# One transfer, one high part, one low part and one release for each 1 MB weight piece, in place of two halves

## What is computed

```
for l in range(2):                                    # first kind
    h = rms_norm(x, norm1_g[l])
    q, k, v, gu, gv = split(h @ w_in[l])              # 2048 x 3584
    mixed = concat(window attention of q, k, v; spatial gating of gu, gv)
    x = x + mixed @ w_o[l]                            # 2048 x 2048
    x = x + (silu(g) * u) @ w_down[l]                 # 5632 x 2048
        # g, u = split(depthwise_conv(rms_norm(x) @ w_up[l]))   2048 x 11264
# second kind, once: modulation rows from silu(c) @ w_ada (2048 x 12288),
# h @ w_in_2, a Hyena branch (FFT convolution) and an SSD scan,
# @ w_out_2, then relu(n @ w_mlp1)^2 @ w_mlp2 with 8192 hidden features
```

## Time and profile before

| | |
|---|---|
| three runs, median (lowest to highest) | 3502.82 us (3501.29 to 3503.66) |
| profiled execution, its own time | 3501.27 us |
| span of the profile | 3499.5 us |
| PE busy | 3407.4 us, 97% of the span, 15842 matmuls |
| DVE busy | 2373.2 us, 68% |
| ACT busy | 1618.5 us, 46% |
| read from HBM | 689.15 MB, 199 GB/s over the span |

### The profile page before, as it was taken

How to read it: one execution, slowest core, us unless ns; L and a number is a source line. 1 busy time by engine, 2 the same in 40 slices (tenths; PEclk the granted TensorE clock), 3 DMA queues, 4 the chain that set the end, 5 groups by cost and what they waited for, 6 DMA issues and landing times.

```text
span 3499.5 us, 43122 instructions
## 1 busy us (share of the span) xinstructions
PE 3407.4 (97%) x15842; PEld 2805.7 (80%) x15842; DVE 2373.2 (68%) x2974; ACT 1618.5 (46%) x2146; POOL 32.5 (1%) x28
## 2 busy tenths in 40 slices
PE   8999999999999999999999999999999999999998
PEld 6888888887778888888887887777866788888886
DVE  5667888888666666777777676676676655556565
ACT  5555555455334555555555444234432544444443
POOL 0000000000000000000000000000000000000000
PEclk9999999999999999999999999999999999999999
DMA  7557777776677557777777773346603566666664
GB/s 256 147 178 222 222 224 228 228 223 217 223 227 222 150 177 220 223 228 232 233 229 239 256 247 113 101 150 198 216 19 127 168 215 207 210 207 214 200 221 156
DMA packets 369459, 697.56 MB, mean 199 GB/s; under 512 B 25487, under 2 KB 37792, under 8 KB 368672
## 3 DMA queue, kind: packets, MB, share of 16 engines
q1 hardware_dynamic: 368628, 695.25, 62.9%
q10 hardware_dynamic: 684, 0.28, 0.0%
HBM read 689.15 MB, written 6.29 MB: 199 GB/s over the span
## 4 chain that ended last, share of the span: by engine, by line
PE 64%; issue 22%; DVE 6%; DMA 3%; ACT 2%; DVEq 2%; ACTq 0%; POOL 0%; SPq 0%; POOLq 0%
PE acc L2185 16%; PE acc L2187 16%; PE acc L2186 16%; PE acc L2473 3%; PE acc L2475 3%; PE acc L2474 3%; DMA w_raw<-in_w_down 2%; DVE w_lo L1320 2%; PE turn L2395 1%; DVE ada_sum L1424 1%; PE turn L2206 1%; PE turn L2222 1%; ACT w_hi L825 1%; DVEq L1416 1%; PE acc L2685 1%
## 5 line engine op out<-in xcount | busy, mean ns | idle before, releaser
L1320 DVE TENSOR_TENSOR w_lo<-w_raw,w_hi 128x1024 fp32r<-128x1024 f32 x708 | 838.4, 1221 | 372.9 <-ACT w_hi L825 336.2
L825 ACT ACTIVATE w_hi<-w_raw 128x1024 fp32r<-128x1024 f32 x708 | 739.0, 1062 | 718.2 <-DMA w_raw<-in_w_up 317.4
L2185 PE MATMUL acc<-w_hi,in_h 128*128 128x512 f32 x1408 | 552.7, 393 | 0.0
L2187 PE MATMUL acc<-w_hi,in_l 128*128 128x512 f32 x1408 | 548.6, 390 | 0.0
L2186 PE MATMUL acc<-w_lo,in_h 128*128 128x512 f32 x1408 | 548.1, 389 | 0.0
L2124 DVE TENSOR_TENSOR w_lo<-w_raw,w_hi 128x1024 fp32r<-128x1024 f32 x252 | 303.4, 1223 | 196.1 <-ACT w_hi L1284 186.3
L1284 ACT ACTIVATE w_hi<-w_raw 128x1024 fp32r<-128x1024 f32 x252 | 265.0, 1060 | 332.2 <-DMA w_raw<-in_w_mlp 331.6
L2473 PE MATMUL acc<-w_hi,in_h 128*128 128x512 f32 x992 | 394.7, 398 | 8.4 <-DVE in_l L2100 4.3
L2474 PE MATMUL acc<-w_lo,in_h 128*128 128x512 f32 x992 | 388.3, 391 | 0.8 <-issue 0.8
L2475 PE MATMUL acc<-w_hi,in_l 128*128 128x512 f32 x992 | 388.5, 392 | 0.0
L1424 DVE SCALAR_TENSOR_TENSOR ada_sum<-w_raw,silu_c,ada_sum 128x512 f32<-128x512 f32 x450 | 327.6, 750 | 31.0 <-issue 7.0
(11 more groups left out here) (365 smaller groups left out, 4714.6 us busy)
## 6 DMA issues: line engine op xcount, KB each, us to landing
w_raw<-in_w_up SPq DMA_DIRECT2D x352, 512.0 KB, 3.8
w_raw<-in_w_mlp SPq DMA_DIRECT2D x256, 512.0 KB, 3.7
w_raw<-in_w_in SPq DMA_DIRECT2D x200, 512.0 KB, 3.7
w_raw<-in_w_ada SPq DMA_DIRECT2D x192, 512.0 KB, 4.2
w_raw<-in_w_down SPq DMA_DIRECT2D x176, 512.0 KB, 5.0
w_raw<-in_w_o SPq DMA_DIRECT2D x64, 512.0 KB, 3.7
w_raw<-in_w_out SPq DMA_DIRECT2D x32, 512.0 KB, 3.9
K<-k_store SPq DMA_DIRECT2D x16, 256.0 KB, 6.5
```

Of the source, the lines that this page charges most:

```text
L825: nc.scalar.activation(hi[s][:, ks], raw[s][:, ks], ACT.Copy).then_inc(w_hi[s][h], 1)
L1320: nc.vector.tensor_tensor(lo[s][:, ks], raw[s][:, ks], hi[s][:, ks].bitcast(F32), ALU.subtract).then_inc(w_lo[s][h], 1)
L2185: nc.tensor.matmul(acc[p][i][:], high(kt)[:, tok], hi[s][:, k], start=(kt == first), stop=False)
L2187: last = nc.tensor.matmul(acc[p][i][:], low(kt)[:, tok], hi[s][:, k], start=False, stop=(kt == final))
```

## The change

Each slot has one semaphore of each kind. A piece is loaded by one transfer of 1 MB, its high part is one ACT instruction of 128x2048 elements, its low part one DVE instruction of 128x2048, PE waits once ahead of the 24 matmuls and releases the slot once behind them. DVE's ada work still stands in two halves at the same two visits, but both wait for, and the slot is released with, the whole piece. The matmuls and their order are the same. (The small dt piece keeps two transfers.)

```diff
-    w_loaded = [[sem(f"w_loaded{s}_{h}") for h in range(2)] for s in range(NS)]
+    w_loaded = [sem(f"w_loaded{s}") for s in range(NS)]
...
         def piece(src, s, r, n=4):
-            for h in range(2):
-                ks = slice(2 * h, min(2 * h + 2, n))
-                sp.wait_ge(w_free[s][h], r)
-                sp.dma_start(raw[s][:, ks], src[:, ks]).then_inc(w_loaded[s][h], 16)
+            sp.wait_ge(w_free[s], r)
+            sp.dma_start(raw[s][:], src).then_inc(w_loaded[s], 16)
...
         def split_hi(s, r, n=4):
-            for h in range(2):
-                ks = slice(2 * h, min(2 * h + 2, n))
-                act_.wait_ge(w_loaded[s][h], r * 16)
-                nc.scalar.activation(hi[s][:, ks], raw[s][:, ks], ACT.Copy).then_inc(w_hi[s][h], 1)
+            act_.wait_ge(w_loaded[s], r * 16)
+            nc.scalar.activation(hi[s][:], raw[s][:], ACT.Copy).then_inc(w_hi[s], 1)
...
         def split_lo(s, r, n=4):
-            for h in range(2):
-                ks = slice(2 * h, min(2 * h + 2, n))
-                dve.wait_ge(w_hi[s][h], r)
-                nc.vector.tensor_tensor(lo[s][:, ks], raw[s][:, ks], hi[s][:, ks].bitcast(F32), ALU.subtract).then_inc(w_lo[s][h], 1)
+            dve.wait_ge(w_hi[s], r)
+            nc.vector.tensor_tensor(lo[s][:], raw[s][:], hi[s][:].bitcast(F32), ALU.subtract).then_inc(w_lo[s], 1)
...
             for k in range(2 * half, 2 * half + 2):
                 dve.drain()
-                if k == 2 * half:
-                    dve.wait_ge(w_loaded[s][half], r * 16)
+                if k == 0:
+                    dve.wait_ge(w_loaded[s], r * 16)
...
-            a.then_inc(w_hi[s][half], 1)
-            dve.drain().then_inc(w_lo[s][half], 1)
-            dve.sem_inc(w_free[s][half], 1)
+            if half == 1:
+                a.then_inc(w_hi[s], 1)
+                dve.drain().then_inc(w_lo[s], 1)
+                dve.sem_inc(w_free[s], 1)
...
-                if k % 2 == 0:
-                    pe.wait_ge(w_lo[s][k // 2], r)
+                if k == 0:
+                    pe.wait_ge(w_lo[s], r)
...
-                if k % 2 == 1:
-                    last.then_inc(w_free[s][k // 2], 1)
+            last.then_inc(w_free[s], 1)
```

More of the change, by code:

```diff
@@ L284, in program @@
     t_free = [sem(f"t_free{b}") for b in range(2)]
+    dt_loaded = sem("dt_loaded")
     x_in, ctx_loaded = [sem(f"x_in{c}") for c in range(4)], sem("ctx_loaded")
@@ L730, in _ @@
                 s, r = ring(FIRST[j])
-                for h in range(2):
-                    sp.wait_ge(w_free[s][h], r)
-                    sp.dma_start(dt_view(raw[s], h), w_in_b[h * D // 2:(h + 1) * D // 2, col:col + 32].rearrange("(k p) n -> p k n", p=P)).then_inc(w_loaded[s][h], 16)
+                sp.wait_ge(w_free[s], r)
+                for h, done in enumerate((w_loaded[s], dt_loaded)):
+                    sp.dma_start(dt_view(raw[s], h), w_in_b[h * D // 2:(h + 1) * D // 2, col:col + 32].rearrange("(k p) n -> p k n", p=P)).then_inc(done, 16)
                 filter_moves(FIRST[j])
@@ L1116, in split_hi2 @@
             s, r = ring(n, q)
-            for h in range(2):
-                act_.wait_ge(w_loaded[s][h], r * 16)
-                v = (lambda w: dt_view(w, h)) if n == FIRST[DT] else lambda w: w[:, 2 * h:2 * h + 2]
-                nc.scalar.activation(v(hi[s]), v(raw[s]), ACT.Copy).then_inc(w_hi[s][h], 1)
+            act_.wait_ge(w_loaded[s], r * 16)
+            if n == FIRST[DT]:
+                act_.wait_ge(dt_loaded, 16)
+                for h in range(2):
+                    a = nc.scalar.activation(dt_view(hi[s], h), dt_view(raw[s], h), ACT.Copy)
+            else:
+                a = nc.scalar.activation(hi[s][:], raw[s][:], ACT.Copy)
+            a.then_inc(w_hi[s], 1)
         def square_sum2(src, dst):
@@ L1281, in hidden @@
                     s, r = ring(mlp_product(n + 2), q)
-                    for h in range(2):
-                        act_.wait_ge(w_loaded[s][h], r * 16)
-                        nc.scalar.activation(hi[s][:, 2 * h:2 * h + 2], raw[s][:, 2 * h:2 * h + 2], ACT.Copy).then_inc(w_hi[s][h], 1)
+                    act_.wait_ge(w_loaded[s], r * 16)
+                    nc.scalar.activation(hi[s][:], raw[s][:], ACT.Copy).then_inc(w_hi[s], 1)
                 if n % NS == 1 and 1 <= n // NS <= 4:
@@ L1364, in _ @@
         for s in range(NS):
-            for h in range(2):
-                dve.sem_inc(w_free[s][h], 1)
+            dve.sem_inc(w_free[s], 1)
         for s in (*acc_free, *t_free, act_s, ada_mod, gate_rows):
@@ L1755, in split_lo2 @@
             s, r = ring(n)
-            for h in range(2):
-                dve.wait_ge(w_hi[s][h], r)
-                v = (lambda w: dt_view(w, h)) if n == FIRST[DT] else lambda w: w[:, 2 * h:2 * h + 2]
-                nc.vector.tensor_tensor(v(lo[s]), v(raw[s]), v(hi[s]).bitcast(F32), ALU.subtract).then_inc(w_lo[s][h], 1)
+            dve.wait_ge(w_hi[s], r)
+            if n == FIRST[DT]:
+                for h in range(2):
+                    a = nc.vector.tensor_tensor(dt_view(lo[s], h), dt_view(raw[s], h), dt_view(hi[s], h).bitcast(F32), ALU.subtract)
+            else:
+                a = nc.vector.tensor_tensor(lo[s][:], raw[s][:], hi[s][:].bitcast(F32), ALU.subtract)
+            a.then_inc(w_lo[s], 1)
         def diagonal(r):
@@ L2120, in hidden @@
                     s, r = ring(mlp_product(n + 2), q)
-                    for h in range(2):
-                        ks = slice(2 * h, 2 * h + 2)
-                        dve.wait_ge(w_hi[s][h], r)
-                        nc.vector.tensor_tensor(lo[s][:, ks], raw[s][:, ks], hi[s][:, ks].bitcast(F32), ALU.subtract).then_inc(w_lo[s][h], 1)
+                    dve.wait_ge(w_hi[s], r)
+                    nc.vector.tensor_tensor(lo[s][:], raw[s][:], hi[s][:].bitcast(F32), ALU.subtract).then_inc(w_lo[s], 1)
                 if n % NS == 1 and 1 <= n // NS <= 4:
@@ L2493, in product_dt @@
                         last.then_inc(done, 1)
-                last.then_inc(w_free[s][h], 1)
+            last.then_inc(w_free[s], 1)
         def turn_dt():
```

51 lines of the change are left out of this document (25 added, 26 removed).

## The result

The changed kernel takes 3623.02 us (median of 4 runs, 3621.72 to 3623.4), the kernel before 3503.24 us on the same chip (4 runs, 3501.29 to 3504.02): ratio 1.0342, 95% interval 1.0329 to 1.0354. It is slower by 120 us, where 68 were forecast, and 3623 lies above the range of 3530 to 3612.

The account below looks back on a forecast made before the run. PE, busy 97% of the span, bounds the kernel by its matmuls. Terms 27 + 22 + 5.5 + 6 + 1.9 (start) + 6 = 68 us on 3501.3 give 3570, median 3571 us; range 3530 to 3612.

Parts of the forecast that it names:

- some 60 us: Sign in PE's table of waits: waiting behind DVE's low part would total some 60 us instead of 8.5.
- The link: Way from an ada piece's end to the low part taking its slot: 6.6 us before, 9.9 forecast, 3.3 more.
- Layer 0, down: 27: Layer 0's down stage: five links 16.5 us, entry 3.5, two of three links in c = 3 give 7.
- Layer 1, down: 22: Layer 1's down stage: rounds longer than PE's matmuls cost 19 us, less about 3, plus 6 in c = 3.
- Where DVE hands over half by half: 5.5: PE starts 1.1 us later, five times in layer 0's up loop (5.5); second block's inputs and MLP start add 6.
- Clock: 6: Slow matmuls after about seven new long waits: 1.5 us for eight, counting at some four places, 6 us.
- The MLP, the o stage and the layers' input products have mostly over 4 us in hand: Cover claimed for those stages, read piece by piece off the timelines; no loss was priced for them there.
- Layer 1's up loop: Low parts done 0.1 to 1 us before PE asks; expected no longer than before.
- rival C: 3598 to 3650 us: burst loads delay each other (+18), layer 1's up loop tips over (20). Chance 0.09.
- What would have made the prediction wrong by its own words: Down stages lengthening by less than 30 us, or up loops by more than 15.

Follow-up runs that it names:

- e4: Kernel before with only PE's wait whole: it waits for both halves' low parts ahead of a piece's matmuls; 3520.1 us, 1.0047.
- e5: Changed kernel with act conversions (ah, al) or accumulator additions put ahead of the last split or low part at three stage entries; 3602.6 us, 1.0288.
- e6: Kernel before (halves) with the same other order at the three entries as e5; 3494.9 us, 0.9976.
- e13: Changed kernel with the first three turns of PE's MLP loop written out, other engines keeping their loops; 3612.3 us, 1.0308.
- e12: Kernel before (halves) with e6's order at the entries and both ada halves of the down stages at the first one's visit; 3487.3 us, 0.9960.
- e14: e12 with the first three turns of PE's MLP loop written out; 3488.0 us, 0.9950.
- e16: Kernel before in quarters instead of halves, with e6's entry order, both ada halves at once and PE's MLP loop written out; 3485.4 us, 0.9953.
- e17: e16 without the change of the ada halves: quarters, entry order, PE's MLP loop written out; 3486.9 us, 0.9954.

## Why the prediction was off

**Direction, and the mechanism in the down stages: right.** The whole piece's way is longer, rounds of ada work are longer than PE's matmuls, and PE waits for low parts: 60.0 us, where "some 60 us" was forecast. The link's 3.3 us more came as 2.8 (load 5.1 for the forecast's 5.3; high part 1.92 for 2.0; low part 2.29 for 2.35). The Trainium skill's 6.15 us for 1 MB (DMA: Bandwidth & Descriptors, section "Measured (HBM→SBUF, 128 partitions, SWDGE, issued from GpSimd)") is for transfers issued from GpSimd; issued from SP it is 5.1 here, from issue to landing. One reading was wrong without a term resting on it: of the four waits that the prediction puts in c = 1, two (934.35 and 938.80) lie there and two (at 971.55 and 977.57, the second in the earlier trace rows) in c = 2.

**"Layer 0, down: 27" and "Layer 1, down: 22": right as pauses.** PE's pauses within the stages grew by 23.8 and 22.6 us (without those at the three entries), 46 in all against 49.

**"Where DVE hands over half by half: 5.5" and 6: right in place, a third too large in the changed kernel.** Layer 0's up loop has the five pauses, each 1.05 us in e4 but 0.7 to 1.0 in the changed kernel, 3.8 in all; its 7.2 us in the table have the entry's 1.6 and 1.8 of matmuls further apart besides. The second block has 3.8 us of such handovers.

**The term that was mis-sized is "Clock: 6".** The measured loss is 53 us over the sum of 68; by kind, 27 of them are here. Busy time of PE grew by 33 us. Counted as stretches of five or more matmuls that stand over 0.35 us apart with no pause between them, there are 31 in the changed kernel and 20 before, and they cost 75 and 50 us over the 0.227 us pitch: 25 of the 33. Most pauses of 2 to 6.5 us are followed by 6 to 13 such matmuls, 1.2 to 2.7 us; not all are, as the two of 2.1 us at the MLP's third turn show. I had counted seven new places, let them vanish at three, and priced eight slow matmuls by the one row after 3.00 us; longer pauses also lengthened stretches that were there before, as from 8 to 12 slow matmuls at layer 1's `down` entry and at the second block's. In the down stages alone it is 20 us.

**The step that failed is the cover: "The MLP, the o stage and the layers' input products have mostly over 4 us in hand".** By place, 38 of the 53 us lie outside the down stages (51 in the table, 13 forecast); this and the clock are two views of one loss and do not add. I had read only how early a product's own low part was. What PE waited for at these places was something else: at three entries `al` or an accumulator behind a late low part in DVE's queue (7.9 us more pause; e5 and e6 put 13 us on it with the slow matmuls); in the second block the filters' steps on DVE (16.9 us for 11.7 before) and late low parts beside them (5.6 us in three pauses, none before); in the layers' input products the copies of `qkT` on ACT (8.1 for 5.0), which I take for the same mechanism by their place in ACT's queue, without an experiment; in the MLP the fetch behind the load (5.5 of 7.9 us more pause; e13, without the jump, gives 8.9 of the 11.5 us back, slow matmuls and the short pauses of before included).

**Layer 1's up loop** was named as the place where rival C would tip. It did not: 3.1 us more, 2.9 of them the pause at the loop's exit. Nor did loads delay each other by 6.7 us. C's size came true by other means, which is luck for C.

**The sum again.** Forecast: 62 us of pauses and 6 of clock. Measured: 88 and 33. Pauses: down stages 46, entries 8, handovers in layer 0's up loop 4, the second block's inputs 14 with its filters, less its entry, which is in the 8, MLP 8, start 2, `qkT` 3, the rest 3. What would have made the prediction wrong by its own words (down stages under 30, up loops over 15) did not occur; the bounds left out the places that I had set at zero.

The version that beats both kernels is halves with the order of the entries and the ada halves at once (e12, 3487 us, 0.4% faster than before by the interval above; e14, e16 and e17 are no better that can be told).
